# Hybrid decoder layer on eight cores: the causal mask by a VectorE minimum on P instead of a TensorE matmul on the scores, and a changed plan around it

## The reference

```python
h = rmsnorm(x, norm_mix_pre);  proj = h @ w_in          # q | k | v | u, 512 columns each
q, k = rope(q), rope(k)                                 # 8 heads x 64
# MoBA attention: keys in blocks of 256. A query sees its own block, causally,
# and the 3 fully past blocks with the largest q . mean(k over block).
s_own = where(kpos <= qpos, q . k * scale, NEG_INF)
p = softmax([s_selected, s_own]);  y_attn = p @ v
y_pool = pool_mixer(u)                                  # trailing means, linear map
x = x + rmsnorm([y_attn, y_pool] @ w_out, norm_mix_post)
a = causal_conv3(rmsnorm(x, norm_ffn_pre) @ w_up)       # 2 x 2816 columns
x = x + rmsnorm((silu(gate) * val) @ w_down, norm_ffn_post)
```

## Time and profile before

| what | value |
|---|---|
| median of 3 runs | 788.35 us (787.2 to 789.49) |
| profiled execution, its own time | 786.13 us |
| span of its slowest core, first to last instruction | 784.6 us (the eight: 781.5 to 784.6) |
| mean granted TensorE clock of the cores | 0.994 to 0.998 |
| TensorE busy | 747.5 us, 95% |
| VectorE, ScalarE, POOL busy | 467.5, 388.4, 281.9 us |

### The profile page before, as it was taken

The page is one execution under the profiler, slowest core; times in us unless marked ns, Lnnn a source line. Parts: engine busy times, 40 slices in busy tenths (PEclk is TensorE's granted clock), DMA queues, the critical chain, the costliest instruction groups (busy, mean ns, idle before and its releaser), DMA issues.

```text
span 784.6 us, 14577 instructions; the slowest of 8 cores (781.5 to 784.6 us)
## 1 busy us (share of the span) xinstructions
PE 747.5 (95%) x4724; PEld 374.9 (48%) x4724; DVE 467.5 (60%) x682; ACT 388.4 (50%) x629; POOL 281.9 (36%) x312
## 2 busy tenths in 40 slices
PE   2899899999999999999999999999999999999995
PEld 1375444556565664444444444444444444444442
DVE  4867766635464446677787772332777877872222
ACT  5476443578798997355554451111445444441111
POOL 1442452220334545366665562100343444330000
PEclk9999999999999999999999999999999999999999
DMA  8999982137349567949897657162444444002321
GB/s 257 312 260 255 167 166 71 42 35 124 102 117 214 150 184 137 192 94 195 157 197 131 119 105 113 55 213 109 108 81 81 71 70 77 1 0 80 109 81 54
DMA packets 65098, 99.72 MB, mean 127 GB/s; under 512 B 38016, under 2 KB 43904, under 8 KB 64000
## 3 DMA queue, kind: packets, MB, share of 16 engines
q1 hardware_dynamic: 52336, 66.01, 31.4%
q0 software_dynamic: 12688, 32.77, 25.6%
HBM read 100.99 MB, written 16.78 MB: 150 GB/s over the span
## 4 chain that ended last, share of the span: by engine, by line
PE 88%; DVE 3%; DMA 3%; issue 2%; ACT 2%; POOL 0%; SPq 0%; DVEq 0%; POOLq 0%; ACTq 0%
PE ps L879 37%; PE ps L962 19%; PE ps L773 8%; PE ps L831 7%; PE ps L708 6%; PE ps L613 5%; PE ps L791 4%; DMA MEM<-w_up_r 1%; PE ps L778 1%; DMA MEM<-x 1%; DMA MEM<-MEM 1%; DVE MEM L524 1%; DVE MEM L620 1%; PE ps L736 1%; SPq L160 0%
## 5 line engine op out<-in xcount | busy, mean ns | idle before, releaser
L879 PE MATMUL ps<-MEM 128*128 128x512 bf16 x1408 | 306.3, 379 | 2.8 <-DVE MEM L840 1.1
L879 PEld LDWEIGHTS ps<-MEM 128*128 128x128 bf16 x1408 | 137.2, 98 | 169.1 <-issue 5.4
L889 ACT ACTIVATE MEM<-ps,MEM 128x1024 f32<-128x1024 f32 x88 | 105.9, 1204 | 140.6 <-PE ps L879 138.0
L787 ACT ACTIVATE MEM<-ps 128x512 bf16<-128x512 f32 (+1 forms) x320 | 147.6, 544 | 33.8 <-PE ps L773 14.0
L962 PE MATMUL ps<-MEM 128*128 128x512 bf16 x704 | 152.3, 379 | 0.0
L915 POOL TENSOR_TENSOR MEM<-MEM 128x1024 bf16<-128x1024 f32 x44 | 103.4, 2351 | 124.2 <-DVE MEM L902 81.2
L892 DVE SCALAR_TENSOR_TENSOR MEM<-ps,MEM 128x1023 f32<-128x1023 f32 x88 | 112.7, 1282 | 51.9 <-ACT MEM L889 51.3
L895 DVE SCALAR_TENSOR_TENSOR MEM<-ps,MEM 128x1022 f32<-128x1022 f32 x88 | 112.6, 1280 | 8.0
L962 PEld LDWEIGHTS ps<-MEM 128*128 128x128 bf16 x704 | 68.9, 98 | 83.1
L773 PE MATMUL ps<-MEM 72*128 72x512 bf16 (+1 forms) x320 | 101.3, 348 | 4.1 <-DMA MEM<-MEM 2.0
L546 POOL TENSOR_SCALAR MEM<-MEM 128x1 f32<-128x1 f32 x63 | 12.1, 191 | 196.9 <-ACT MEM L970 118.8
(11 more groups left out here) (88 smaller groups left out, 586.5 us busy)
## 6 DMA issues: line engine op xcount, KB each, us to landing
MEM<-w_up_r POOLq DMA_DIRECT2D x44, 512.0 KB, 6.1
MEM<-x SPq DMA_DIRECT2D x32, 512.0 KB, 5.8
x1s<-MEM SPq DMA_DIRECT2D x16, 512.0 KB, 3.9
MEM<-x1s SPq DMA_DIRECT2D x16, 512.0 KB, 5.3
out<-MEM SPq DMA_DIRECT2D x15, 512.0 KB, 2.6
MEM<-w_down POOLq DMA_DIRECT2D x22, 256.0 KB, 7.3
MEM<-w_qk SPq DMA_DIRECT2D x4, 1024.0 KB, 14.8
MEM<-w_vu SPq DMA_DIRECT2D x4, 1024.0 KB, 20.7
```

Of the source, the lines that this page charges most:

```text
L787: op("act", lambda e, c0=c0, u=u, p=p: e.activation(out=PT[p][:, c0:512], in_=bk[u.ids[0]][:, c0:512], func=AF.Exp, scale=SCALE), rd=u.b, ...
L879: mm = op("pe", lambda e, c=c, half=half, pr=pr, ws=ws, tb=tb: e.matmul(bk[pr.ids[tb]], lhsT=wu[ws][:, c, half * 128:(half + 1) * 128], rh ...
L889: op("act", lambda e, pr=pr, ch=ch, ts=ts: e.activation(out=tA[ts], in_=ps(pr)[:, :], func=AF.Identity, scale=cwb[:, ch, 2:3], bias=cwb[:, ...
```

## The change

Four things.

1. The mask matmul L778 is gone. On a diagonal tile, after exp, VectorE takes the minimum of the 128x128 diagonal block of P (bf16) with a table that now holds 0 above the diagonal and 3.0e38 elsewhere, in place. A second buffer name, `PD`, stands for that block: only the one PV matmul of the tile that reads the block waits for VectorE, the other PV matmuls wait for exp alone, as before. The plan costs the minimum with n=240.
2. Up-weight slots 0 and 1 now lie in the query buffer of group 2, slots 2 and 3 in the pool mixer's space; slots 4 and 5 stay.
3. The first matmul of the first two units waits for the last output-projection matmul of tile 7, and the second 512-token half of a unit starts only after its first half has.
4. The plan's DMA times for the first microseconds are changed: rate factor 0.8 in place of 0.7 and first latency 2.2 in place of 3.0 before 3 us, and a factor 0.78 for SP's queue where its line stands between 31 and 52 us.

```diff
-                rate = self.CAST if o["cast"] else self.RATE * (0.7 if t < 3.0 else 1.0)
+                rate = self.CAST if o["cast"] else self.RATE * (0.8 if t < 3.0 else 1.0)
+                if e == "sp" and 31.0 < line[e] < 52.0:
+                    rate *= 0.78
...
-                    line[e] = max(line[e], t + (1.2 if t > 3.0 else 3.0)) + ...
+                    line[e] = max(line[e], t + (1.2 if t > 3.0 else 2.2)) + ...
...
-        wu = [... for a in (aPL, aPL + 1024, aQT, aQT + 1024, aPT, aPT + 1024)]
+        wu = [... for a in (aQT, aQT + 1024, aPL, aPL + 1024, aPT, aPT + 1024)]
...
-                                            rhs=QT[G % 2][0:72, h, c0:512], start=True, stop=(nd < 0)),
+                                            rhs=QT[G % 2][0:72, h, c0:512], start=True, stop=True),
...
-                if nd >= 0:
-                    op("pe", lambda e: e.matmul(bk[u.ids[0]][:, c0:c0 + 128], lhsT=ident, rhs=tri, start=False, stop=True),
-                       rd=[buf("cst")], wp=u.b, n=128)
...
-                   rd=u.b, wr=[buf("PT%d" % p)], n=512 - c0)
+                   rd=u.b, wr=[buf("PT%d" % p), buf("PD%d" % p)], n=512 - c0)
+                if kt >= 4 * G:
+                    op("dve", lambda e, c0=c0, p=p: e.tensor_tensor(out=PT[p][:, c0:c0 + 128], in0=PT[p][:, c0:c0 + 128], in1=tri,
+                                                                  op=ALU.min), rd=[buf("cst")], wr=[buf("PD%d" % p)], n=240)
...
-                       rd=[buf("PT%d" % p), VA_b[kt], buf("VAones%d" % (kt // 8))], ...)
+                       rd=[buf("%s%d" % ("PD" if kt - 4 * G == qb else "PT", p)), VA_b[kt], buf("VAones%d" % (kt // 8))], ...)
...
-                               deps=unit + (last_exp if 4 <= u < 8 else []) if c == tb == 0 else (),
+                               deps=unit + (last_exp if 4 <= u < 8 else []) + ([sec_mm[7]] if u < 2 else []) if c == tb == 0 else ([lead] if c == 0 else ()),
...
-        wu_alias[0] = union(["poolc"])
-        wu_alias[1] = union(["ur%d" % i for i in range(5)])
+        wu_alias[2] = union(["poolc"])
+        wu_alias[3] = union(["ur%d" % i for i in range(5)] + ["df0", "df1"])
...
-        wu_alias[2] = wu_alias[3] = q_al[0]
+        wu_alias[0] = wu_alias[1] = q_al[0]
...
-    idtri[:, 1, :] = np.where(tp > t, NEG, 0.0)
+    idtri[:, 1, :] = np.where(tp > t, 0.0, 3.0e38)
```

More of the change, by code:

```diff
@@ L247, in schedule @@
                 else:
-                    line[e] = max(line[e], t + (1.2 if t > 3.0 else 3.0)) + o["nbytes"] / (rate * (0.6 if busy else 1.0))
+                    line[e] = max(line[e], t + (1.2 if t > 3.0 else 2.2)) + o["nbytes"] / (rate * (0.6 if busy else 1.0))
                     fin = max(line[e], free_at[e] + 0.8) + 0.8
@@ L414, in build @@
         PT = [b16v(aPT + i * 256, 256) for i in range(8)]
-        wu = [b16v(a, 1024).rearrange("p (c n) -> p c n", c=8) for a in (aPL, aPL + 1024, aQT, aQT + 1024, aPT, aPT + 1024)]
+        wu = [b16v(a, 1024).rearrange("p (c n) -> p c n", c=8) for a in (aQT, aQT + 1024, aPL, aPL + 1024, aPT, aPT + 1024)]
         aCS = carve(128)
@@ L793, in attn @@
                         start=(kt == 0 and qb == 0), stop=(kt == nkt - 1)),
-                       rd=[buf("PT%d" % p), VA_b[kt], buf("VAones%d" % (kt // 8))], n=64, **W(kt == 0 and qb == 0, pb.b[0]))
+                       rd=[buf("%s%d" % ("PD" if kt - 4 * G == qb else "PT", p)), VA_b[kt], buf("VAones%d" % (kt // 8))], n=64, **W(kt == 0 and qb == 0, pb.b[0]))
                 if n + 2 < N:
@@ L824, in build @@
         last_sec = []
+        sec_mm = {}
         def sec1(tt):
@@ L835, in sec1 @@
             last_sec[:] = [mm]
+            sec_mm[tt] = mm
             xb, nb, xsb = buf("xn%d" % (tt % 2)), buf("n1a%d" % (tt % 2)), buf("xs%d" % s)
@@ L876, in up_section @@
                     ch = p + NPAIR * half
+                    lead = None
                     for c in range(8):
@@ L883, in up_section @@
                                rd=[buf("wu%d" % ws)] + hT2_b[8 * g + 4 * tb:8 * g + 4 * tb + 4],
-                               deps=unit + (last_exp if 4 <= u < 8 else []) if c == tb == 0 else (),
+                               deps=unit + (last_exp if 4 <= u < 8 else []) + ([sec_mm[7]] if u < 2 else []) if c == tb == 0 else ([lead] if c == 0 else ()),
                                **W(c == 0, pr.b[tb]))
                             first = first or mm
+                            lead = mm if c == tb == 0 else lead
                     unit = [mm]
@@ L1056, in build @@
             buf("PT%d" % i).r = union(["xn2", "xn3"])
+            buf("PD%d" % i).r = union(["xn2", "xn3"])
         for i in range(2):
@@ L1089, in build @@
         attn(3, lambda h: sec1(4 + h))
-        wu_alias[0] = union(["poolc"])
-        wu_alias[1] = union(["ur%d" % i for i in range(5)])
+        wu_alias[2] = union(["poolc"])
+        wu_alias[3] = union(["ur%d" % i for i in range(5)] + ["df0", "df1"])
         q_al = [union(["QT%d_0" % s, "QT%d_1" % s, "QTm%d" % s]) for s in range(2)]
         st_al = union(["stg%d_%d" % (i, j) for i in range(3) for j in range(2)])
-        last_exp = union(["PT%d" % i for i in range(8)])
+        last_exp = union(["PT%d" % i for i in range(8)] + ["PD%d" % i for i in range(8)])
         pt_al = last_exp
-        wu_alias[2] = wu_alias[3] = q_al[0]
+        wu_alias[0] = wu_alias[1] = q_al[0]
         wu_alias[4] = wu_alias[5] = pt_al
```

## The result

The changed kernel takes **808.12 us** (median of 4 runs, 805.22 to 919.02), the kernel before on the same chip 788.92 us (787.2 to 791.01). The ratio is 1.0231, 95% interval [1.0187, 1.0275]: slower by 2.3%, where I forecast 781.8 us and faster. In some executions of every kernel here one half of the chip (four cores) works at a lower clock and takes longer, as in that of 919.02 us: the ratios leave such executions out, the medians don't, and where single spans are compared, they are those of the half that isn't slowed. The profiled execution took 807.16 us, its span is 805.6 us; the eight cores span 798.3 to 805.6 us at mean clocks of 0.982 to 0.988.

What follows compares the result with a forecast made beforehand. TensorE's own work was taken to bound the kernel. Masks at -7.3 us and waits for the minimum at +0.7 summed to -6.6 us, taken from the median 788.35 to 781.8 us; range 778.5 to 787.5 us.

Steps and rivals of the forecast that it cites:

- Masks, -7.3 us: Attention on TensorE: 128 removed mask matmuls at 0.057 us each save 7.3 us.
- my lower bound of 6.4: Attention on TensorE: smallest saving from the masks, 128 matmuls at 0.05 us each, 6.4 us.
- My sign of "busy time down by about 7 us": Whole kernel: TensorE's busy time was to fall by about 7 us if the forecast held.
- The rival that exp becomes the bound: Late attention: with ScalarE full, the masks of groups 2 and 3 gain nothing; gain 2.9 us, 785.4 us, chance 0.14.
- Minimum, 26 us of VectorE: Attention: 128 minima at 0.20 us add 26 us (9 to 44) to VectorE, within its free time, costing nothing.
- Waits for the minimum, +0.7 us: Attention: PV matmuls wait 0.006 us for each of 128 minima, +0.7 us; bounds 0 and +10.
- The slower rival: Attention: minima stand behind 1.28 us VectorE operations and TensorE waits, 10.2 us lost; 791.3 us, chance 0.10.
- Moved work, 0: Preparation, group 1's scores, hand-over and weight slots: reordered work and changed DMA figures cost 0 in sum.
- the hand-over at +2.8 us: Hand-over, 305 to 339 us: 2.8 us idle before, change taken as 0, bounds -2.8 and +2.8.
- The line of the DMA wait ahead of group 1's scores: Ahead of group 1's scores: wait and low clock, together 3.5 us, kept unchanged at 0; bounds -3.5 and +3.5.
- My own list of marks: Signs set beforehand; waits for VectorE above 5 us in attention or a hand-over above 5 us idle would disprove the forecast.

Runs made afterwards that it cites:

- g1: Changed kernel with the second section's residual addition on VectorE, old DMA figures, tile 12's output projection behind 192 up matmuls: 790.04 us, 0.9974; again 796.41 us, 0.9986.
- e4: Changed kernel, same plan, the minimum replaced by a one-operand maximum over the same block, diagonal causal mask left out: 800.47 us, 1.0138.
- f4: Changed kernel with the second section's residual addition moved from GpSimd to VectorE: 799.45 us, 1.0109.
- f3: Changed kernel with the 1024-column residual addition on GpSimd issued as four of 256 columns: 808.4 us, 1.0187.
- g5: Changed kernel with the minimum on PSUM scores ahead of exp, additions on GpSimd, old DMA figures, tile 12 behind 192 up matmuls: 791.03 us, 0.9993.
- the hold: Tile 12's output projection held back: behind 128 up matmuls in the changed kernel, 806.01 us; behind 192 with mask matmuls put back, 791.86 us.
- e2: Kernel before with the change's slots, two added dependences and DMA figures, mask matmuls kept: 800.88 us, 1.0127.

## Why the prediction was wrong

**Masks, -7.3 us: too high, and not collected.** They are gone. What that is worth on TensorE can be read from all twenty kernels: its busy time, with the stretches at a lower clock counted by the clock's share, is 744.0 to 744.6 us (mean of the eight cores) in the five that have mask matmuls and 739.4 to 741.4 in the fifteen that don't; for the kernel before and the changed one 744.6 and 740.6. That is 4.0 us in place of 7.3, below my lower bound of 6.4. (Gaps shorter than the modelled overlap of two matmuls count as busy, so some of the rest may be small stalls in the place of the masks; what takes it was not shown.) My sign of "busy time down by about 7 us" did not come true.

In g1, where the three causes are mended, even these are given back. On core 4, g1's first row against that of the kernel before, 110 to 220 us:

```profile
110.00:220.00 110.00, 106.14 (x976) 57.82 (x974) 70.16 (x221) 75.59 (x162) 20.44 (x27) 0.98 0.37 80
```

```profile
110.00:220.00 110.00, 108.66 (x1060) 62.15 (x1059) 62.73 (x174) 70.78 (x152) 28.67 (x31) 1.00 0.39 83
```

2.5 us more of idle time, and a stretch of 3.4 us at 1.2 GHz, 1.7 us of clock. From 60 to 365 us this core has 11.2 us idle against 7.6; with the clock that is 5.3 us, and its span is 782.0 us against 781.5. The rival that exp becomes the bound named this kind of end (2.9 us of gain left); that exp is what takes it was not shown.

**Minimum, 26 us of VectorE: right in the median, wrong as a sum.** 0.22 us against my 0.20; but 42.9 us of busy time in all, since 8 of 128 took 2.25 to 2.85 and one 0.97.

**Waits for the minimum, +0.7 us: this step failed first.** It measured 9.9 us, and taking the cause away was worth 7 us (e4) to 9 us (f4). I carried over the rate of 320 exp waits, 0.006 us each. The waits for exp stayed at 1.9 us; a two-operand SBUF operation on VectorE is held up by POOL, and no row of exp could tell of that. The slower rival had the right size (10.2 us) from a wrong cause: it feared VectorE's own 1.28 us operations, which the plan knows, and not POOL, whose hold on VectorE no cost in the plan contains. I gave it 0.10, arguing that VectorE is half idle. An idle share says nothing of an engine that is held up.

The kernel before showed it, from the other side. Its timelines of VectorE and POOL:

```profile
297.53 1.28 DVE L848 SCALAR_TENSOR_TENSOR MEM<-MEM 128x1024 bf16<-128x1024 f32 x1
...
297.75 3.26 POOL L843 TENSOR_TENSOR MEM<-MEM 128x1024 f32<-128x1024 f32 x1 [1.83 <-DVE MEM L840]
```

L843 takes 2.35 us alone; here it starts 1.06 us before L848 is done and takes 3.26. The Trainium skill states the rule in "SBUF — State Buffer", section "SBUF: two separate sides": a VectorE operation with two SBUF inputs and a GpSimd operation that reads SBUF exclude each other, and whoever starts first has the ports for its whole instruction. These rows, seven of the eight long minima, e4, f3 and g5 agree with it. The longest one, 2.85 us, agrees less well: its row starts 0.3 to 0.4 us ahead of the addition's, while POOL issues a weight load, and it too ends with the addition. Minima beside such an issue alone take 0.21 to 0.23 us, so it isn't the issue that holds them; why this one was held so early was not shown. I had weighed only pages on rates and fixed costs.

**Moved work, 0: failed too.** I bounded the hand-over at +2.8 us, by its idle time, and noted tile 12's earlier `sec1` in the order without asking what it reads. It reads the last transposed y, which can be issued only behind the last PV matmul. The transposition was no short one before either: 12.3 to 15.2 us on the eight cores, and it landed 15.9 to 18.4 us behind the last PV matmul; in the changed kernel it takes 14.5 to 16.7 us and lands 17.6 to 19.9 us behind it. What changed is the cover. Of the 117 matmuls 12 stood ahead of the last PV matmul, so 105 covered the transposition, 22.7 us; of the 96 now 33 do, so 63 are left, 13.6 us. Both counts stand in the order that I had ahead of me. In the changed kernel the hold is worth 2 to 3 us of time, in e2 9 (800.9 to 791.9, on two chips).

**DMA figures: also in the 0.** The line of the DMA wait ahead of group 1's scores was bounded at +3.5 us. The wait itself grew by 1.4 us between the slowest cores; but a second low-clock stretch came at 72 to 80 us, where 68 to 72 us has 1.4 us of idle time between scores, exp and PV matmuls with no projection matmul to fill. Put back alone: 3 to 4 us.

**The sum, redone.** The causes sit in different stretches, so the traces themselves add up. The changed kernel against the one before, TensorE, mean of the eight cores in us:

| stretch | idle time | lost clock | what lies there |
|---|---|---|---|
| 0 to 60 | +0.7 | 0 | |
| 60 to 110 | +2.0 | +5.0 | the DMA figures' stretch at half clock |
| 110 to 170 | -0.1 | 0 | |
| 170 to 305 | +8.0 | +2.6 | the long minima |
| 305 to 365 | +4.5 | +1.5 | the hand-over |
| 365 to the end | 0 | +0.1 | |
| masks gone | -4.0 | | |

That is 20.3 us, where the eight spans grew by 19.5 on average (lost clock that falls on idle time is counted twice). That a stretch's loss is its cause's alone is my reading; put in or taken out one at a time, the causes came to 5 to 9, 3 to 4 and 2 to 3 us, each in another plan.

**My own list of marks** was sound: it called waits for VectorE above 5 us, or a hand-over above 5 us idle, the proof against me. The first came true at 9.9 us, and the second at 6.8 us (mean of the cores, 305 to 365 us).

## What to carry to other kernels

When work moves to VectorE, ask what GpSimd does beside it: here a small operation with two SBUF operands lasted as long as the GpSimd instruction that it met, and the end of a VectorE operation that feeds GpSimd is where they meet. Give one operand from PSUM, shorten the GpSimd instruction, or move it. In a kernel whose order a planner makes, price every pull-forward by what it reads, DMA landing times above all, and count the cover from the instruction that lets the transfer start; and when a change loses more than its terms allow, hold single instructions back before arguing about the rest.

## What the runs showed of the hardware

A minimum of 128 columns takes 0.22 us, 2.25 to 2.85 beside a GpSimd addition of 2.35 us, 0.8 to 1.3 beside GpSimd operations of 1.27 us, and still 0.22 while GpSimd issues a DMA; with one SBUF operand (0.28 and 0.29 us in the median) the longest of 128 was 0.29 and 0.30. A 128 KB transposing DMA, 4.2 us from issue to landing in the median, took 12.3 to 15.2 us at the hand-over of the kernel before, 14.5 to 16.7 in the changed one and up to 24.3 in e2, each time with weight loads under way; that the loads are what slows it was not tested. Without the 128 mask matmuls TensorE's busy time at full clock is 4 us shorter, 0.03 us each, where 0.057 us lay between one's start and the next.
